# Half the frequencies of a real Fourier transform in a float32 transformer kernel, with the weight rows k and 128-k mixed on POOL

## What is computed

```python
def fourier_mix(a):
    ag = a.astype(jnp.float32).reshape(Bsz, S, 8, 128)      # 8 groups of 128 channels
    y = jnp.fft.fftn(ag, axes=(1, 3), norm="ortho").real    # over tokens and a group's channels
    return y.reshape(Bsz, S, 1024)
...
y_a = fourier_mix(a_in) @ w_br_a[l]
y_b = dilated_mixture(qb, kb, vb, ...) @ w_br_b[l]
y_c = diff_attention(qc, kc, vc, ...) @ w_br_c[l]           # dense attention, 4 heads x 2 maps
gates = jax.nn.sigmoid(u @ w_gate[l] + b_gate[l])           # three gates of width 1024
merged = gates_a * y_a + gates_b * y_b + gates_c * y_c
x = x + merged @ w_out[l]
```

## Time and profile before

| | |
|---|---|
| median of 3 runs | 3368.24 us (3367.11 to 3368.75) |
| the profiled execution, its own time | 3366.69 us |
| its span in the profile | 3364.9 us |
| PE busy | 3326.8 us (99%) |
| PEld busy | 2732.9 us (81%) |
| DVE busy | 1459.0 us (43%) |
| ACT busy | 1358.5 us (40%) |
| POOL busy | 1570.9 us (47%) |
| DMA | 93 GB/s mean |

### The profile page before, as it was taken

How to read it: one execution, slowest core, us unless ns; L and a number is a source line. 1 busy time by engine, 2 the same in 40 slices (tenths; PEclk the granted TensorE clock), 3 DMA queues, 4 the chain that set the end, 5 groups by cost and what they waited for, 6 DMA issues and landing times.

```text
span 3364.9 us, 53294 instructions
## 1 busy us (share of the span) xinstructions
PE 3326.8 (99%) x17098; PEld 2732.9 (81%) x17098; DVE 1459.0 (43%) x2273; ACT 1358.5 (40%) x2440; POOL 1570.9 (47%) x1210
## 2 busy tenths in 40 slices
PE   8999999999999999999999999999999999999999
PEld 7888888788888888888888788888877787788887
DVE  5223622655322342324534645232468776342324
ACT  4323324654432343324235634332347654343333
POOL 4544443245454445444533264544433457255444
PEclk9999999999999999999999999999999999999999
DMA  3333322233232333333322232333322223123322
GB/s 126 109 96 97 118 87 68 74 104 99 96 108 97 97 98 107 98 96 115 100 75 77 64 119 94 111 96 96 96 88 63 62 65 109 54 84 109 96 96 88
DMA packets 176397, 313.88 MB, mean 93 GB/s; under 512 B 19188, under 2 KB 30452, under 8 KB 176264
## 3 DMA queue, kind: packets, MB, share of 16 engines
q1 hardware_dynamic: 171824, 302.24, 28.2%
q10 hardware_dynamic: 4440, 9.87, 1.1%
HBM read 309.88 MB, written 2.15 MB: 93 GB/s over the span
## 4 chain that ended last, share of the span: by engine, by line
PE 94%; DVE 3%; issue 1%; POOL 1%; ACT 1%; DMA 0%; ACTq 0%; SPq 0%; DVEq 0%; POOLq 0%
PE ps L691 25%; PE ps L693 25%; PE ps L692 25%; PE ps L730 2%; PE ps L732 2%; PE ps L731 2%; PE ps L967 1%; PE ps L712 1%; PE ps L714 1%; PE ps L713 1%; PE ps L982 1%; PE ps L1166 1%; PE ps L1455 0%; PE ps L847 0%; PE ps L974 0%
## 5 line engine op out<-in xcount | busy, mean ns | idle before, releaser
L555 POOL TENSOR_TENSOR w_lo<-raw,w_hi 128x512 fp32r<-128x512 f32 x1120 | 1488.7, 1335 | 1709.8 <-ACT w_hi L1515 1705.2
L1515 ACT ACTIVATE w_hi<-raw 128x512 fp32r<-128x512 f32 x1120 | 693.8, 628 | 1291.8 <-PE ps L693 1187.0
L691 PE MATMUL ps<-u_hi,w_hi 128*128 128x512 f32 (+1 forms) x2870 | 1123.3, 391 | 5.3 <-DVE u_lo L3143 4.0
L693 PE MATMUL ps<-u_lo,w_hi 128*128 128x512 f32 (+1 forms) x2870 | 1111.7, 387 | 0.0
L692 PE MATMUL ps<-u_hi,w_lo 128*128 128x512 f32 (+1 forms) x2870 | 1111.1, 387 | 0.0
L691 PEld LDWEIGHTS ps<-u_hi,w_hi 128*128 128x128 f32 x2870 | 539.6, 188 | 123.0 <-issue 8.7
L693 PEld LDWEIGHTS ps<-u_lo,w_hi 128*128 128x128 f32 x2870 | 539.5, 188 | 110.8
L692 PEld LDWEIGHTS ps<-u_hi,w_lo 128*128 128x128 f32 x2870 | 539.9, 188 | 110.1 <-issue 2.9
L2273 DVE TENSOR_TENSOR T<-ps,rs 128x512 f32<-128x512 f32 x268 | 184.9, 691 | 723.0 <-PE ps L693 721.2
L691 PE MATMUL ps<-m_hi,w_hi 128*128 128x512 f32 x948 | 372.1, 392 | 2.4 <-DVE m_lo L2685 1.3
L692 PE MATMUL ps<-m_hi,w_lo 128*128 128x512 f32 x948 | 368.9, 389 | 0.0
(11 more groups left out here) (517 smaller groups left out, 3180.2 us busy)
## 6 DMA issues: line engine op xcount, KB each, us to landing
raw<-jobs SPq DMA_DIRECT2D x1120, 256.0 KB, 2.7
tab<-vec_in ACTq DMA_DIRECT2D x8, 448.0 KB, 5.5
pt<-rows_dram SPq DMA_DIRECT2D x9, 256.0 KB, 5.0
x<-x_in SPq DMA_DIRECT2D x4, 512.0 KB, 6.9
out<-x SPq DMA_DIRECT2D x16, 128.0 KB, 1.9
tab<-dft_in ACTq DMA_DIRECT2D x2, 901.0 KB, 4.7
pt<-share_dram ACTq DMA_DIRECT2D x4, 384.0 KB, 4.7
T<-rows_dram SPq DMA_DIRECT2D x3, 256.0 KB, 6.5
```

The lines of the kernel that those rows point to most:

```text
L555: pool.tensor_tensor(w_lo[:, s, w], raw[:, s, w], w_hi[:, s, w].bitcast(F32), ALU.subtract).then_inc(lo_done[s], 1)
L691: pe.matmul(ps[bank][:, 0:n], w_hi[:, s, w], hi[:, k, 0:n], start=k == ks[0], stop=False)
L693: last = pe.matmul(ps[bank][:, 0:n], w_hi[:, s, w], lo[:, k, 0:n], start=False, stop=k == ks[-1])
L1515: act.activation(w_hi[:, s, half_of(half)], raw[:, s, half_of(half)], ACT.Copy).then_inc(hi_done[s], 1)
```

## The change

Only the frequencies 0 to 64 of each group are computed. `along_channels(j)` now does two groups at once, with cosine tables of 65 columns and sine tables of 64, and `along_tokens(j)` runs four times and not eight; its output, cosine part in columns 0 to 256 and sine part in 257 to 511, is not unfolded but goes straight to `m_hi` and `m_lo`. Frequency 64, which has no partner, is carried for all eight groups as 8 rows (`highest_along_tokens`, `highest_hi`, `highest_lo`). The projection then needs two sets of weights: rows k plus rows 128-k for the cosine part, their difference for the sine part. The host writes rows k in the first half of a job and rows 128-k in the second; POOL makes difference and sum.

```diff
+            def mirrored_low(i):
+                for s in range(2):
+                    ahead, back = raw[:, s, half_of(0)], raw[:, s, half_of(1)]
+                    for half in range(2):
+                        pool.wait_ge(raw_full[s][half], 16 * (i + 1))
+                    pool.tensor_tensor(differences[s], back, ahead, ALU.subtract)
+                    pool.tensor_tensor(ahead, ahead, back, ALU.add).then_inc(mixed[s], 1)
+                    pool.wait_ge(hi_done[s], i * 2 + 1)
+                    low(s, 0)
+                    pool.wait_ge(hi_done[s], i * 2 + 2)
+                    w = half_of(1)
+                    pool.tensor_tensor(w_lo[:, s, w], differences[s], w_hi[:, s, w].bitcast(F32), ALU.subtract).then_inc(lo_done[s], 1)
...
-            def half_job(s, half, hi, lo, ready):
+            def mirrored_job(s, half, m, ready):
...
+                cs = slice(0, FOLDED) if half == 0 else slice(S // 2, S)
+                o = ps[s if half == 0 else 5][:, cs]
+                if half == 1:
+                    pe.wait_ge(pv_copied, c.now("pv_copied"))
+                for k in range(KT // 2):
...
+                    pe.matmul(o, w_hi[:, s, w], m_hi[:, k, cs], start=k == 0, stop=False)
+                    pe.matmul(o, w_lo[:, s, w], m_hi[:, k, cs], start=False, stop=False)
+                    last = pe.matmul(o, w_hi[:, s, w], m_lo[:, k, cs], start=False, stop=half == 1 and k == KT // 2 - 1)
...
+                    pe.matmul(o, highest_hi[:, m // 4, w], hi, start=False, stop=False)
+                    pe.matmul(o, highest_lo[:, m // 4, w], hi, start=False, stop=False)
+                    pe.matmul(o, highest_hi[:, m // 4, w], lo, start=False, stop=True).then_inc(job_half[s], 1)
```

```diff
+            def unfolded(m):
+                s = m % 2
+                p, q, y = ps[s], odd_part, in_order
+                dve.wait_ge(job_done[s], c.next(f"job{s}"))
+                dve.wait_ge(odd_copied, c.next("odd_copied"))
                 dve.tensor_copy(y[:, 0:HALF:2 * P], p[:, 0:EVEN:P])
...
+                dve.tensor_tensor(y[:, 2:HALF - 1:2], p[:, 1:P], q[:, 0:P - 1], ALU.add)
+                dve.tensor_tensor(y[:, S - 2:HALF - 1:-2], p[:, 1:P], q[:, 0:P - 1], ALU.subtract)
+                dve.tensor_tensor(y[:, 1:HALF - 1:2], p[:, EVEN:HALF], q[:, P - 1:S - HALF], ALU.add)
+                dve.tensor_tensor(y[:, S - 1:HALF - 1:-2], p[:, EVEN:HALF], q[:, P - 1:S - HALF], ALU.subtract).then_inc(evac[s], c.up(f"evac{s}"))
+                dve.wait_ge(evac[s], c.now(f"evac{s}"))
+                dve.wait_ge(silu_done, c.next("silu"))
+                dve.tensor_tensor(pt[:, m], pt[:, m], y, ALU.mult)
...
-                        dve.tensor_tensor(pt[:, m], pt[:, m], ps[m % 2][:, :], ALU.mult).then_inc(evac[m % 2], c.up(f"evac{m % 2}"))
+                        unfolded(m)
...
+                    if u % 2:
+                        s = u // 2 % 2
+                        act.wait_ge(job_done[s], c.now(f"job{s}"))
+                        act.wait_ge(evac[1 - s], c.now(f"evac{1 - s}"))
+                        act.activation(odd_part, ps[5][:, HALF:S], ACT.Copy).then_inc(odd_copied, c.up("odd_copied"))
```

More of the change, by code:

```diff
@@ L156, in constants @@
     odd_sin[0] = 1 - 2 * (j[:P] % 2)
[L157 to L161, removed]
+    signs = np.broadcast_to(1 - 2 * (j % 2), (P, EVEN))
+    c["dft"] = np.concatenate([np.cos(a[:, :FREQ + 1]) / 256, np.sin(a[:, :FREQ]) / 256, np.cos(even), np.cos(odd),
+                               even_sin, odd_sin, signs], 1)
     c["eye"] = np.eye(P)
@@ L843, in fourier, with along_channels @@
             def fourier():
[L844 to L848, removed]
-                    mm.then_inc(z_full, c.up("z_full"))
+                def along_channels(j):
+                    pe.wait_ge(z_act, c.take("z_act"))
+                    for part in range(2):
+                        for e in range(2):
+                            at = (2 * part + e) * (FREQ + 1)
+                            pe.matmul(ps[2][:, at:at + FREQ + 1], pt[:, 2 * j + e, part * P:part * P + P], dft_c, start=True, stop=True)
+                    for part in range(2):
+                        for e in range(2):
+                            at = (2 * part + e) * FREQ
+                            mm = pe.matmul(ps[3][:, at:at + FREQ], pt[:, 2 * j + e, (2 + part) * P:(3 + part) * P], dft_s, start=True, stop=True)
+                    mm.then_inc(z_full, c.up("z_full"))
@@ L882, in fourier @@
                         mm.then_inc(vt_full, c.up("vt_full"))
[L883 to L893, removed]
+                    if g % 2 == 0:
+                        along_tokens(g // 2)
+                highest_along_tokens()
             def v_tiles(g):
@@ L1520, in pump, with mirrored_split @@
                 split(s, 1)
+            def mirrored_split(s, half):
+                if half == 0:
+                    c.up(f"raw{s}", 16)
+                    act.wait_ge(mixed[s], c.next(f"mixed{s}"))
+                    act.wait_ge(job_half[s], c.take(f"half{s}"))
+                else:
+                    act.wait_ge(job_done[s], c.take(f"slot{s}"))
+                act.activation(w_hi[:, s, half_of(half)], differences[s] if half else raw[:, s, half_of(0)], ACT.Copy).then_inc(hi_done[s], 1)
             def skip(s):
@@ L1693, in dense @@
                     act.activation(T[:, 4 + u % 2], ps[4][:, :], ACT.Copy).then_inc(tr_copied, c.up("tr_copied"))
-                    split(1 - u // 2 % 2, u % 2)
+                    if u < 14:
+                        mirrored_split(1 - u // 2 % 2, u % 2)
+                    else:
+                        split(0, u % 2)
                     if u % 2:
```

209 lines of the change are left out of this document (126 added, 83 removed).

## The result

The changed kernel takes 3375.68 us (median of 20 runs, 3372.32 to 3378.39); the kernel before, on the same chip, 3368.79 us (20 runs, 3366.59 to 3371.60). The ratio is 1.0020, with a 95% interval of 1.0013 to 1.0027: slower by 0.2%. The forecast was 3375 us.

What follows compares the result with a forecast made beforehand. PE was taken to bound the kernel, with DVE about as slow in the dense stage and setting its pace afterwards. Per layer, -4.95 us (Fourier) and +8.5 us (dense) gave +7 us in all, 3375 us; range 3354 to 3389 us.

Steps and rivals of the forecast that it cites:

- What bounds the kernel now: Whole kernel: PE is 94% of the chain, but the dense stage is balanced, PE's turn 10.3 us, DVE's 8.3 bare.
- The ring: Dense stage: DVE and PE wait for each other in turns of two slots; after the change DVE sets the pace.
- Projection on PE: Dense stage: a job's two halves take 3.8 us instead of 5.7, 1.95 less; PE's turn becomes 8.4 us.
- Fourier stage: Fourier stage on PE: four of eight along_tokens go, frequency 64 adds 1.06 us; 4.95 us a layer saved.
- Unfolding on DVE: Dense stage: DVE's turn grows by 1.15 us, to 9.4 us bare, and DVE sets the pace.
- Twice the work on POOL: Dense stage: POOL's operations hold up DVE's softmax operations, 1.3 us a pair, seven pairs, 9 us a layer.
- The ring by itself: Dense stage without any contention, unfolding included: 87.5 us a layer, against 88.0 before.
- The sum: Dense stage 87.5 + 9 = 96.5 us, 8.5 longer; with Fourier's -4.95, +3.5 us a layer, +7 us in all.
- Rival 4: Dense stage: PE's clock falls through its waits, +5 us a pair, 3440 us or more; chance 0.05.
- case 1: Dense stage: DVE bounds it and POOL holds it up by 0.8 to 2.2 us a pair, 3368 to 3388 us; chance 0.65.
- Rival 2: Dense stage: POOL and DVE miss each other, contention below 0.8 us a pair, 3354 to 3368 us; chance 0.25.
- Rival 3: Whole kernel: PE stays the bound and all its savings are kept, 41 us, 3327 us; chance 0.05.

Runs made afterwards that it cites:

- no_mixing_no_unfolding: The changed kernel without POOL's difference and sum and without DVE's five small unfolding operations (output not the reference's); 3354.1 us, ratio 0.9958.
- before_moved: The kernel before, with DVE's multiplication of the projection moved ahead of the logits in even slots; 3367.6 us, ratio 1.0000.
- no_mixing: The changed kernel without POOL's difference and sum, rows split as they come (output not the reference's); 3365.8 us, ratio 0.9990.
- busy_gaps: The changed kernel with eight more unused matmuls of 256 columns at the end of each slot, in PE's idle time; 3374.3 us, ratio 1.0015.
- placed: The changed kernel with POOL's difference and sum one per slot, each waiting for the end of DVE's softmax; 3364.7 us, ratio 0.9988.
- the best order: The changed kernel with unfolding and multiplication moved ahead of the logits in even slots and POOL's difference and sum after the softmax; 3348.9 us, ratio 0.9943.
- no_unfolding: The changed kernel without DVE's five small unfolding operations, POOL's difference and sum kept (output not the reference's); 3363.6 us, ratio 0.9985.
- late_split: The changed kernel with unfolding ahead of the logits, POOL's mixing after the softmax, and ACT's odd-slot split after the two exponentials; 3353.2 us, ratio 0.9958.

## Why the prediction was right, and where it was not

The time, the sign and the case were right. That the time is right within 1 us is partly luck, as the point on the ring by itself shows. Step by step:

- *What bounds the kernel now.* Right. The ring set the length of the stage: no_mixing_no_unfolding still has 85.8 us of it, with PE's work cut by 15%, and before_moved shows that PE bounds it before the change.
- *Projection on PE.* Right: a half of 15 matmuls takes 2.19 us (661.46 to the values at 663.65) and one of 12 takes 1.51 us (666.19 to 667.70), 3.7 us for the 3.8 forecast.
- *Fourier stage.* Right: 5.3 and 5.6 us for 4.95.
- *Unfolding on DVE*, 1.15 us on each of seven turns, 8 us a layer: half of the 12.1 us that leaving it out gained is 6, and half of the 11.7 between no_mixing and no_mixing_no_unfolding is the same, so it was oversized by 2.
- *Twice the work on POOL.* The sum of 9 us a layer agrees with the stretch of 9.2. Its make-up does not: the forecast had 0.26 us on the one-number operation and 1.05 on the softmax in each pair. Measured were 15 x 0.29 = 4.4 us on the first, from the low parts, and 4.8 on the second. (The forecast also had the multiplication meet nothing; it is stretched by 1.1 us, in the last pair.) By the run that left it out, the mixing costs 5 us a layer.
- *The ring by itself* was taken too short. The forecast's 87.5 us without contention hold 8 us of unfolding, so 79.5 us without either burden; no_mixing_no_unfolding has 85.8 us, 3.2 of them stretch, so about 82.6. These 3 us too few were made good by the 2 too many of the unfolding and by a sum of contention that was up to 1 us too large (3.2 + 5 for 9). The terms missed in both directions and cancelled: a luck of some 3 us a layer. (The 23.0 us for pairs 1 and 2 come to 22.8 by the forecast's own terms, which changes nothing.)
- *The sum* of a dense stage, 96.5 us, is what busy_gaps has (96.6, with 0.95 of its own work). The changed kernel itself has 100.2 and 98.1, and the term that was missing is the clock. *Rival 4* said that a fall of the clock would cost 5 us a pair and end at 3440 us, and got 0.05. The clock did fall, but only behind the longest gaps of this kernel (2.06 to 2.79 us), in three or four of the seven pairs, for 3 to 4 us at a time, and made the wait for the scores 1.0 to 1.4 us longer each time. I had priced it as all or nothing, where it was a small part of case 1. The profiled execution lies 4 us above the 3373.8 us that the sum gave for it; the median lies lower and met 3375 us.
- *Rival 2* (the engines miss each other) did not come about by itself; two waits on POOL brought it about in placed. *Rival 3* was wrong for the changed kernel and is mostly wrong even in the best order, where 20 of its 41 us came out.

What stays open is what the low clock costs in a typical execution, and when it falls. The two layers of one profile differ in where it falls and by 2.1 us in length, so a number from one profile is no more than an example. The length of a single gap does not decide it: in layer 2 of no_unfolding the clock stayed at 1.00 behind a gap of 2.07 us (1854.80), and in layer 2 of placed it fell behind one of 1.36 us (1906.04). Open too is why the ring by itself takes 3 us more than its turns add up to.

## What to carry to other kernels

Work that is taken from the engine with the largest busy share pays only as far as the ring around it lets go: count each engine's turn, its fixed waits too, before pricing the saving. Where new work must go on another engine of the ring, look first for the place where that engine waits for the ring itself (here 2 us for the scores, which held the whole unfolding), and tie POOL's operations by one wait each to the end of DVE's operations with two inputs in SBUF, so that they run in the gaps between them. Moving one operation may only shift the meeting to the next one, as late_split did. The same instructions in another order were worth 27 us here, the change itself 7 in the other direction.

## What was not expected of the hardware

- In the changed kernel PE's granted clock fell to its lower level behind single gaps of 2 to 3 us and was back at 1.00 within 4 us. Eight matmuls without a use in each slot kept it at 1.00.
- The block between POOL and DVE works in both directions and passes on: a side operation on DVE held POOL for 0.7 us, POOL then held the one-number operation (0.22 us of work took 1.04) and the softmax (0.75 took 1.72), and the softmax held POOL's sum (1.26 took 1.71).
- A 0.22 us operation on one number for each row is as easily held up as one on 512: up to 1.34 us.
